# Query rotations between weight splits, attention rows out of PSUM by ScalarE alone, and the last columns and norm token by token

## The reference

```python
# block one
proj = rmsnorm(x, norm_mix_g) @ w_in             # latents, differential q, k, v, gates
q = rmsnorm(q_lat, g) @ mla_w_uq                 # 8 heads, 64 plain + 32 rotated columns
kv = rmsnorm(kv_lat, g) @ mla_w_ukv
o_mla = causal_attention(q_mla, k_mla, v_mla)    # 8 heads, values of 64 columns
o_diff = rmsnorm(o1 - lam * o2, g)               # 4 differential heads
x = x + (g_mla * (o_mla @ w_branch_mla) + g_diff * (o_diff @ w_branch_diff)) @ w_out
x = x + (silu(hn @ w_ffn_gate) * (hn @ w_ffn_up)) @ w_ffn_down
x = rmsnorm(x, norm_final_g)
# block two
q, k, v, za, u, vs, zs, gm = split(rmsnorm(x, norm_g_2) @ w_in_2)
q, k = partial_rope(q), partial_rope(k)          # 16 query heads, 2 key heads
a = (window_sink_attention(q, k, v, sinks) * silu(za)) @ w_att_out
sgo = (chunked_spatial_gating(gelu(u), gelu(vs)) * silu(zs)) @ w_sg_out
y = sigmoid(ga) * a + sigmoid(gs) * sgo
x = x + y @ w_o
out = x * rsqrt(mean(x * x) + eps) * final_g     # the last norm, over 1024 columns
```

## Time and profile before

| | us |
|---|---|
| median of 3 runs | 1302.12 (1301.53 to 1302.45) |
| profiled execution, whole time | 1302.51 |
| profiled execution, span from first to last instruction | 1300.8 |
| TensorE busy in the span | 1274.4 (98%) |
| VectorE, ScalarE, GpSimd busy | 700.1, 527.8, 55.1 |
| TensorE waits for `w_lo` (line 1150), all | 5.2 in 4 waits, the longest 4.1 |
| TensorE waits for `om_lo` (line 1430), all | 2.5 in 3 waits |

### The profile page before, as it was taken

One profiled execution on the slowest core, in us unless ns is written; L12 is line 12 of the kernel. 1 busy time (PEld: TensorE's weight loads), 2 busy tenths in 40 slices (PEclk: granted clock), 3 DMA queues, 4 the chain that ended last, 5 costly groups with the idle time before them and its releaser, 6 DMA issues.

```text
span 1300.8 us, 15821 instructions
## 1 busy us (share of the span) xinstructions
PE 1274.4 (98%) x6212; PEld 1062.9 (82%) x6212; DVE 700.1 (54%) x1073; ACT 527.8 (41%) x889; POOL 55.1 (4%) x97
## 2 busy tenths in 40 slices
PE   8999999999999999999999999899999999999997
PEld 6877778888888888888888888688988888888885
DVE  6776656654545444444433348756555436446554
ACT  5546554652334434343323243336553343223222
POOL 0002231220000000000000000000000000000000
PEclk9999999999999999999999999899999999999999
DMA  6232323123432332323223233231104322322321
GB/s 196 69 97 66 81 74 89 50 81 92 160 120 65 97 100 94 99 95 114 95 91 104 97 98 114 65 97 38 61 1 146 108 91 94 103 92 98 104 75 64
DMA packets 106362, 119.53 MB, mean 92 GB/s; under 512 B 13814, under 2 KB 88636, under 8 KB 106300
## 3 DMA queue, kind: packets, MB, share of 16 engines
q1 hardware_dynamic: 106160, 118.64, 29.1%
q10 hardware_dynamic: 140, 0.04, 0.0%
HBM read 113.42 MB, written 2.10 MB: 89 GB/s over the span
## 4 chain that ended last, share of the span: by engine, by line
PE 89%; DVE 6%; ACT 3%; issue 2%; POOL 1%; DVEq 0%; ACTq 0%; POOLq 0%
PE ps_mm L1930 55%; PE ps_mm L1965 22%; PE ps_o L2342 2%; PE ps_o L2117 1%; ACT w_hi L640 1%; PE ps_s L2094 1%; DVE w_lo L1150 1%; PE ps_t L2322 1%; PE ps_mm L1936 1%; PE ps_mm L2025 1%; PE ps_s L2138 1%; PE ps_t L2104 1%; PE ps_s L2307 1%; PE ps_o L2165 1%; PE ps_s L2305 1%
## 5 line engine op out<-in xcount | busy, mean ns | idle before, releaser
L1930 PE MATMUL ps_mm<-act_hi,w_hi 128*128 128x512 f32 x944 | 373.6, 396 | 5.2 <-DVE w_lo L1150 5.2
L1930 PE MATMUL ps_mm<-act_lo,w_hi 128*128 128x512 f32 x944 | 371.1, 393 | 0.0
L1930 PE MATMUL ps_mm<-act_hi,w_lo 128*128 128x512 f32 x944 | 370.9, 393 | 0.0
L1150 DVE TENSOR_TENSOR w_lo<-stage,w_hi 128x2048 fp32r<-128x2048 f32 (+3 forms) x77 | 157.7, 2048 | 173.9 <-ACT w_hi L640 173.9
L1930 PEld LDWEIGHTS ps_mm<-act_hi,w_hi 128*128 128x128 f32 x944 | 178.0, 189 | 41.5 <-DVE w_lo L1150 6.7
L1930 PEld LDWEIGHTS ps_mm<-act_hi,w_lo 128*128 128x128 f32 x944 | 177.9, 188 | 35.7
L1930 PEld LDWEIGHTS ps_mm<-act_lo,w_hi 128*128 128x128 f32 x944 | 178.0, 189 | 34.4
L640 ACT ACTIVATE w_hi<-stage 128x2048 fp32r<-128x2048 f32 (+3 forms) x78 | 133.1, 1706 | 166.6 <-PE ps_mm L1965 119.1
L1566 DVE TENSOR_TENSOR w_lo<-stage,w_hi 128x2048 fp32r<-128x2048 f32 x23 | 52.7, 2293 | 56.3 <-ACT w_hi L919 56.2
L1965 PE MATMUL ps_mm<-w_hi,h_hi 128*128 128x512 f32 x176 | 68.8, 391 | 0.0
L1965 PE MATMUL ps_mm<-w_hi,act_hi 128*128 128x512 f32 x176 | 68.6, 390 | 0.0
(11 more groups left out here) (389 smaller groups left out, 1973.9 us busy)
## 6 DMA issues: line engine op xcount, KB each, us to landing
stage<-in_w_in SPq DMA_DIRECT2D x44, 1024.0 KB, 5.3
stage<-in_w_ffn_gate SPq DMA_DIRECT2D x11, 1024.0 KB, 5.3
stage<-in_w_ffn_up SPq DMA_DIRECT2D x11, 1024.0 KB, 5.3
stage<-in_w_ffn_down SPq DMA_DIRECT2D x10, 1024.0 KB, 5.0
stage<-in_w_out SPq DMA_DIRECT2D x4, 1024.0 KB, 5.0
stage<-in_w_att_out SPq DMA_DIRECT2D x4, 1024.0 KB, 5.1
stage<-in_w_sg_out SPq DMA_DIRECT2D x4, 1024.0 KB, 5.1
stage<-in_w_o SPq DMA_DIRECT2D x4, 1024.0 KB, 5.2
```

What stands on the lines that cost most here:

```text
L1150: V.tensor_tensor(w_lo[:, s, 0:k * w], stage[:, s, 0:k * w], w_hi[:, s, 0:k * w].bitcast(F32), ALU.subtract).then_inc(w_lo_made, 1)
L1930: ins = T.matmul(ps_mm[:, 2 * bank_slot + m, :], wt[:, kk, m * P:(m + 1) * P], acts[ap][:, kk, :], start=(r == 0), stop=(r == per - 1), sk ...
```

## The change

There are three edits, independent of one another.

1. *First attention.* ScalarE copies a complete head out of `ps_o` into `p2`, a tile in SBUF of the later stage, and this copy alone signals `o_free`. The high part is made by a second ScalarE copy from `p2`, placed behind the exponential of the same step; VectorE's subtraction reads `p2` and is placed behind the scaling of probabilities. A new semaphore `om_made` counts it, and TensorE waits for all eight before the second attention, which uses `p2` again.
2. *Queries.* VectorE's `lo` of units q2 3, kv2 and za 0 moves from in front of a unit's two rotations to between them. `hi` and `lo` of za 1 move ahead of the key copies and the value rows.
3. *The end.* Units wo 2 and 3 are taken token by token: blocks 0 and 1 of wo 2, blocks 0 and 1 of wo 3, block 2 of both, block 3 of both. Each block has its own norm: the sum over the first 512 columns is prepared early, ScalarE takes a square root from its table, VectorE a reciprocal and one Newton step, and each engine scales 512 columns. `hi` of wo 3 stands ahead of the squares of the fourth block.

```diff
@@ ScalarE, first attention
-                    nc.scalar.activation(om_hi[rr, h // 2, :], ps_o[rr, :], ACT.Copy).then_inc(o_hi_made, 1)
+                    nc.scalar.activation(p2[rr, h // 2 % 2, :], ps_o[rr, :], ACT.Copy).then_inc(o_free, 1)
...
+                if p > LAG and (p - LAG - 1) % 4 == 3 and p - LAG - 1 < NP:
+                    act.wait_ge(o_free, h + 1)
+                    nc.scalar.activation(om_hi[rr, h // 2, :], p2[rr, h // 2 % 2, :], ACT.Copy).then_inc(o_hi_made, 1)
@@ VectorE, first attention (moved from ahead of the reciprocal to behind the scaling)
-                    V.tensor_tensor(om_lo[rr, h // 2, :], ps_o[rr, :], om_hi[rr, h // 2, :].bitcast(F32), ALU.subtract
-                                    ).then_inc(o_free, 1)
+                    V.tensor_tensor(om_lo[rr, h // 2, :], p2[rr, h // 2 % 2, :], om_hi[rr, h // 2, :].bitcast(F32),
+                                    ALU.subtract).then_inc(om_made, 1)
@@ ScalarE, block two
+            hi(U0["za"] + 1)
             act.wait_ge(k_roped, 1)
...
-                hi(u + 1)
+                if i:
+                    hi(u + 1)
@@ VectorE, queries
+            for n in range(KD):
+                u, m = U0["q2"] + n // 2, n % 2
+                if n >= 3 and m:
                     lo(u + 2)
+                if n >= 2:
+                    dve.wait_ge(q2_lo_made, 2 * (n - 1))
+                rope_bank(u, m, prob2[:, m, :], rope2, swap8, AD ** -0.5, q2_roped, n + 1)
+                if n:
+                    q_rests(n - 1)
             u = U0["kv2"]
             rope_bank(u, 0, kv[:, 1, :], rope2, swap8, 1.0, k_roped, 1)
             q_rests(7)
+            lo(U0["za"] + 1)
@@ ScalarE, the end
+            nc.scalar.activation(fin_root[:, 4:5], halfpi, ACT.Sqrt)
+            hi(U0["wo"] + 1)
+            hi(U0["wo"] + 2)
+            for t in range(3):
+                fin_squares(0, t)
+            hi(U0["wo"] + 3)
+            fin_squares(0, 3)
+            for t in range(TT):
+                fin_squares(1, t)
+                act.wait_ge(pre_made, 1)
+                nc.scalar.activation(fin_root[:, t:t + 1], part[:, 4 + t:5 + t], ACT.Sqrt, scale=1.0 / D,
+                                     bias=var[:, t:t + 1]).then_inc(fin_rooted, 1)
+                act.wait_ge(x_gained, 12 + t + 1)
+                act.wait_ge(rstd_made, 4 + t)
+                nc.scalar.activation(res[:, t, 0:D // 2], vs[:, t, 0:D // 2], ACT.Copy, scale=rstd[:, t:t + 1]
+                                     ).then_inc(fin_made_act, 1)
@@ VectorE, the end
+            def fin_norm(t):
+                v, y, n = var[:, 4 + t:5 + t], rstd[:, t:t + 1], newton[:, t:t + 1]
+                dve.wait_ge(fin_squared, 4 + t + 1)
+                link(V.scalar_tensor_tensor(out=v, in0=part[:, 4 + t:5 + t], scalar=1.0 / D, in1=var[:, t:t + 1],
+                                            op0=ALU.mult, op1=ALU.add))
+                dve.wait_ge(fin_rooted, t + 1)
+                after(link(V.reciprocal(y, fin_root[:, t:t + 1])))
+                after(link(V.tensor_tensor(n, y, y, ALU.mult)))
+                after(link(V.scalar_tensor_tensor(out=n, in0=n, scalar=-0.5, in1=v, op0=ALU.mult, op1=ALU.mult)))
+                V.scalar_tensor_tensor(out=y, in0=n, scalar=1.5, in1=y, op0=ALU.add, op1=ALU.mult
+                                       ).then_inc(rstd_made, 1)
...
+                V.tensor_scalar(res[:, t, D // 2:D], vs[:, t, D // 2:D], y, None, ALU.mult).then_inc(fin_made, 1)
@@ TensorE, the end
+            for tokens in ((0, 1), (2,), (3,)):
+                for i in (2, 3):
+                    wide_unit(U0["wo"] + i, acts_x, tokens=tokens)
```

More of the change, by code:

```diff
@@ L542, in _ @@
             for t in range(TT):
-                for done, count in scaled_when(t, 1, fin_made, fin_made_act):
-                    sp.wait_ge(done, count)
+                sp.wait_ge(fin_made, t + 1)
+                sp.wait_ge(fin_made_act, t + 1)
                 sp.dma_start(ov[:, t, :], res[:, t, :]).then_inc(out_written, 16)
@@ L711, in scale_tiles @@
                                          ).then_inc(signal, 1)
[L713 to L718, removed]
             def part_squares(i, t, kind, src, out, signal):
@@ L1115, in _, with fin_squares @@
                     nc.scalar.activation(act_hi[:, c, :], gu[:, c, :], ACT.Copy).then_inc(y_hi_made, 1)
[L1116 to L1125, removed]
-                        half_scale(t // 2, 4 + t // 2, res, vs, fin_made_act)
+            def fin_squares(i, t):
+                act.wait_ge(bank_free, freed(U0["wo"] + 2 * i + 1, t))
+                part_squares(i, t, 0, res, tmp[:, t % 2, :], fin_squared)
+                act.wait_ge(fin_squared, 4 * i + t + 1)
+            nc.scalar.activation(fin_root[:, 4:5], halfpi, ACT.Sqrt)
[14 more added lines that the diff above has]
+                                     ).then_inc(fin_made_act, 1)
         @block.vector
@@ L1199, in add_parts @@
                                            AX.X, ALU.add)))
-            def half_norm(m, signal, due, made, out, src, scaled):
-                dve.wait_ge(signal, due)
-                after(link(V.tensor_reduce(ssq[:, 2 * m:2 * m + 2],
-                                           part[:, 0:8].rearrange("p (i t) -> p t i", i=2)[:, 2 * m:2 * m + 2, :],
-                                           AX.X, ALU.add)))
-                rsqrt(2, 1.0 / D, made, 2 * m)
-                for t, n in (((0, 0),), ((2, 0), (3, D // 2)))[m]:
-                    V.tensor_scalar(out[:, t, n:D], src[:, t, n:D], rstd[:, t:t + 1], None, ALU.mult
-                                    ).then_inc(scaled, 1)
             def norm_lo_chunk(row, base, k):
@@ L1439, in _ @@
                                     ).then_inc(p_ready, 1)
+                if p > LAG and (p - LAG - 1) % 4 == 3 and p - LAG - 1 < NP:
+                    h = (p - LAG - 1) // 4
+                    rr = slice((h % 2) * MV, (h % 2) * MV + MV)
+                    dve.wait_ge(o_hi_made, h + 1)
+                    V.tensor_tensor(om_lo[rr, h // 2, :], p2[rr, h // 2 % 2, :], om_hi[rr, h // 2, :].bitcast(F32),
+                                    ALU.subtract).then_inc(om_made, 1)
                 if p == 0:
@@ L1951, in wide_unit @@
                     pe.wait_ge(w_lo_made, u + 1)
-                order = [(t, kk) for t in range(TT) for kk in range(k)]
+                order = [(t, kk) for t in tokens for kk in range(k)]
                 if chunk_waits is not None and first:
@@ L2368, in _ @@
                 straight(U0["sgo"] + i, "F", (at_hi, at_lo))
-            for i in range(4):
-                if i < 2:
-                    pe.wait_ge(y_lo_made, 4 * (i + 1))
+            for i in range(2):
+                pe.wait_ge(y_lo_made, 4 * (i + 1))
                 wide_unit(U0["wo"] + i, acts_x)
+            for tokens in ((0, 1), (2,), (3,)):
+                for i in (2, 3):
+                    wide_unit(U0["wo"] + i, acts_x, tokens=tokens)
 _INS = ["x", "positions", "norm_mix_g", "w_in", "b_gate", "mla_q_norm_g", "mla_w_uq", "mla_kv_norm_g", "mla_w_ukv",
```

42 lines of the change are left out of this document (18 added, 24 removed).

## The result

| | before | after |
|---|---|---|
| median of the runs, us | 1302.28 (1301.53 to 1302.48, 4 runs) | 1290.89 (1290.02 to 1291.13, 4 runs) |
| span of the profiled execution, us | 1300.8 | 1289.3 |
| TensorE busy, us | 1274.4 (98%) | 1271.9 (99%) |

The ratio is 0.9911, with a 95% interval of 0.9899 to 0.9922: 11.4 us faster by the medians. Forecast were 13.1 us less and 1289.1 us, range 1287.0 to 1293.0.

The account below looks back on a forecast made before the run. TensorE, busy 1274.4 of 1300.8 us, was taken as the bound, so only its stalls, slow running and the tail count. 3.5 + 6.6 + 3.0 = 13.1 us off gave 1289.1 us, range 1287.0 to 1293.0.

Parts of the forecast that it names:

- all seven waits go: First attention, head ends: TensorE no longer waits for `ps_o`; 4.1 us were lost there.
- the residual at the seventh head: First attention, seventh head: TensorE waits some 0.5 us for the turned probabilities behind ScalarE's new copy.
- what is late next: First attention: ScalarE's extra 0.6 us copy per head delays only the seventh head; 3.5 us won, bounds 0 to 4.1.
- GpSimd beside the subtraction: First attention: by the skill's rule each subtraction may last up to 1.3 us longer, but the two hardly meet.
- Edit 2: Queries, value rows and za 1: waits and half clock go, 6.8 us, less 0.2 at za 2; 6.6 us won.
- the sign: Queries: `w_lo` of za 1 ready at 4 us or more before its start.
- Edit 3: The end: earlier addition, shorter norm and scaling, one last write; 3.0 us won, bounds 2.5 to 3.5.
- the chance named in the bounds: The end: a lone write lands sooner than 3.1 us, making the gain 3.5 us.
- The table load: Ahead of wo 1's `w_hi`: costs 1.28 us, 4.4 to spare; split keeps 2.9, or 1.5 with the skill's drain.
- the first one: Rival, first attention: ScalarE's second copy and blocked VectorE cost TensorE as much as the 3.5 us; 1292.6 us, chance 0.10.
- No unit of the query stretch was late: Rival, queries: za 1's wait moves to another unit, clock falls again, edit 2 gives nothing; 1295.7 us, chance 0.05.
- no table was switched for a root: Rival, the end: tables switched for every root, two 1.28 us loads on the last chain; 1291.7 us, chance 0.03.

Follow-up runs that it names:

- late high parts: Changed kernel with `om_hi` and `om_lo` of a finished head made one step later: 1289.63 us, ratio 0.9906.
- the last variant with VectorE's rotation: Changed kernel with high parts made a step later, last output block in two writes, last query rotation of the second attention on VectorE: 1288.51 us, ratio 0.9895.
- edit 1 alone: Only the first-attention edit, put on the kernel before: 1300.30 us, ratio 0.9987.
- edit 3 alone: Only the edit of the end, put on the kernel before: 1298.36 us, ratio 0.9970.
- the kernel with the splits in their old place: Changed kernel with rests of q2 3, kv2 and za 0 back ahead of a unit's two rotations, za 1's split staying moved: 1293.58 us, ratio 0.9940.

## Why the prediction was right, and where it was off

- *The way of reading it* (only places where TensorE stands still count, priced by starts) held: from 14.0 us on the whole difference is found at the three places and at the start of the second attention, right behind the first of them; the rest adds up to less than 0.1 us.
- *Edit 1, all seven waits go:* right. Behind every head it is 0.45 us now. Of the 4.1 us so forecast, 3.73 arrived up to the seventh head; at the next two steps behind the sixth head, where the copy of the turned tile stands behind `om_hi` and a key copy, 0.16 and 0.13 us were lost, and with late high parts these are not (3.93). "At the other six I find 0.4 us or more to spare" looked at the wait of the first step only.
- *Edit 1, the residual at the seventh head:* mechanism and place right (a wait for `pt`, behind `om_hi`), size 0.88 instead of 0.5.
- *Edit 1, what is late next:* this is the step that failed. The search stopped at the end of the first attention. TensorE came 2.3 us earlier to its end, and the chain of the last query rotation only 0.2 us: 0.81 us, at no price in the forecast. Edit 1 gave 2.0 us, not 3.5, well inside its bounds of 0 and 4.1 and near neither.
- *GpSimd beside the subtraction:* in the changed kernel all eight subtractions took 0.68 to 0.69 us, and none met GpSimd, as argued. With the high parts late, three of them meet it (the first, the second and the eighth) and took 1.76, 1.66 and 1.67 us; the other five took 0.68 to 0.69. The Trainium skill (GPSIMD Engine Reference, section Specifications) counts instructions with two SBUF inputs among those that contend with GpSimd, and these rows agree. The eighth:

```profile
193.09 1.66 POOL L601 TENSOR_TENSOR dq<-dq,rope_d 128x512 f32<-128x512 f32 x1 [3.44 <-DVE tmp L1447]
...
193.62 1.67 DVE L1438 TENSOR_TENSOR om_lo<-p,om_hi 64x512 fp32r<-64x512 f32 x1
```

- *Edit 2:* 6.8 us instead of 6.6. The waits and the clock gave 7.07 (6.8 forecast), za 2 took back 0.25 (0.2 forecast). VectorE went 10.6 us per unit (10.45 forecast), without a gap. The split of za 1 was ready 3.7 us ahead, not the 4 or more named as the sign.
- *Edit 3:* 3.15 us instead of 3.0, so near only by luck, as two errors cancel. Up to the end of the scaling the forecast had 3.83 us from the last matmul and 3.79 came (the root 0.29 where the earlier trace rows had suggested 0.2). A lone write landed in 2.6 us, not 3.1, the chance named in the bounds; but the forecast had left out the 0.4 us between the last landing and the end of the span. The 6.6 us from the last matmul's end to the landing were 6.1.
- *The table load:* ScalarE's copy ahead of it ends at 1241.45, the load of 1.28 us starts at 1241.47 and the root behind it at 1242.76. At 14 other loads of this trace the next instruction likewise starts 0.01 us behind the load. The trace of the kernel before has 14 such loads too and could have told this ahead of the forecast. The Trainium skill (ScalarE: Activation LUTs, section What ACT_TABLE_LOAD costs) adds a drain of 1.38 us to each switch; none is to be seen here, and the measurement decides.

```profile
1241.47 1.28 ACT L1121 ACT_TABLE_LOAD   x1
1242.76 0.20 ACT L1121 ACTIVATE small<-small 128x1 f32<-128x1 f32 x1
```

- *The sum:* 12.0 us from 14.0 us on, 1.1 short of 13.1: -1.5 for edit 1, +0.2 for edit 2, +0.15 for edit 3. The medians show 11.4; the 0.6 more are of the size of the start's scatter.
- *Rivals:* the first one (the second copy takes the wait's place) came true by half, through a chain it did not name. No unit of the query stretch was late, no table was switched for a root, and nothing was slower.

## What to carry to other kernels

When a wait on the critical engine goes, follow what that engine will ask for next until it meets a chain that did not move with it, past the end of the stage too; a rotation on a slow engine, started by a copy that stands behind your new instruction, is such a chain. An added instruction with no hurry belongs behind every copy that someone waits for, a whole step later if need be. And where several medians differ by less than they scatter, lay the traces beside each other by the bottleneck engine's instructions: here the stretches behind the start repeated within 0.1 us, but for the one in which the clock had fallen, while the whole times scattered by 2.

## What was not expected of the hardware

**The start.** The executions differ mainly in the first 14 us, by -0.47 to +1.82 us against the kernel before over all the traces of this study, in kernels that are the same there. TensorE's matmuls of 512 columns start 0.43 us apart at first, the pace that they have elsewhere at a granted clock of 0.50 (1.2 GHz), and go over to 0.23 at a different time: the first timeline, of the kernel with late high parts, has them at the fast pace at 8.75 us (0.40 us each, not 0.63), the second, of the last variant with VectorE's rotation, still slow at 12.03.

```profile
8.75 0.40 PE L2045 MATMUL ps_mm<-w_hi,act_lo 128*128 128x512 f32 x1
```

```profile
12.03 0.63 PE L2055 MATMUL ps_mm<-w_lo,act_hi 128*128 128x512 f32 x1
...
13.50 0.40 PE L2055 MATMUL ps_mm<-w_hi,act_lo 128*128 128x512 f32 x1
13.73 0.40 PE L2055 MATMUL ps_mm<-w_lo,act_hi 128*128 128x512 f32 x1
```

The windows of the profile show a granted clock of 1.00 for this time too, but that is no measurement: the record of the clock in each trace has its first entry, full speed, only later, at 8.45 us in the first of these two and at 13.21 us in the second. In the first 90 us of all 14 traces no two such matmuls in a row keep the fast pace ahead of this entry, and none the slow one behind it; and from 8.37 us on a later entry always goes with a longer first stretch. So the start's scatter is the time at which the clock rises to full. Why that time varies stays open.

**The clock behind a wait.** After the 4.07 us without work ahead of za 1 TensorE worked at a granted clock of 0.50 from 837.65 to about 842.3 us in the kernel before, 4.6 us, but with edit 1 alone from 835.35 to about 838.6, 3.2 us, and with edit 3 alone from 838.95 to about 844.9, 5.9 us, though the wait was as long each time (4.07 us). These are the -0.64 and +0.58 us of the table. So what that half clock costs is not the same in each execution. After the 2.59 us without work in the kernel with the splits in their old place it stayed at 1.00.

**GpSimd beside VectorE.** A half weight split on VectorE, 128x1024, took 2.04 us beside GpSimd's rotation in the changed kernel and 1.22 us where VectorE did the rotation itself; and GpSimd's second multiplication, 1.3 us in the rotation ahead of it, took 2.16 in that company. Both pay. The kernel before shows the same at this place (2.05 and 2.16 us).
